# Order of the even mixer, low-rank gates in halves, and another bank for late sums in a tuned transformer kernel

## The reference, cut to what matters

```python
def first_block(...):
    layer 0: hn = rms_norm(h); proj = hn @ w_in_e
             a = gmlp_spatial_gate(gelu(a_uv), ...)        # u * (causal w_s @ layer_norm(v) + b_s)
             b = gated_deltanet(qkv, z, beta, a, ...)      # conv, silu, l2-norm of q and k,
                                                           # triangular solve, state over chunks,
                                                           # rms_norm per head, silu(z)
             h += concat([a, b]) @ w_out_e
    layer 1: h += diff_attention(hn @ w_qkv_o, ...) @ w_out_o   # 8 heads, two softmaxes each, norm per head
    each:    h += square(relu(rms_norm(h) @ w_mlp1)) @ w_mlp2
             h += (p @ w_ple_proj) * sigmoid(rms_norm(h) @ w_ple_gate)

def gla_mixer(h, w_in, w_gk_up, b_gk, head_norm, w_out):        # second block, layer 0
    q, k, v, glr, z = split(h @ w_in)                           # glr: 16 columns, the low rank
    gk = log_sigmoid(glr @ w_gk_up + b_gk) / 16                 # 16 x 512
    o = gla_chunked(q, k, v, gk)                                # 4 heads, 256 values each
    return (rms_norm(o, head_norm) * silu(z)) @ w_out
# second block, layer 1: nsa_mixer (untouched)
```

## Time and profile before

| | |
|---|---|
| median of 3 runs | 2063.66 us (2061.76 to 2064.04) |
| time of the profiled execution | 2062.59 us |
| its span | 2060.4 us |
| PE busy | 1980.1 us (96%) |
| DVE, ACT, POOL busy | 1069.3, 891.7, 221.5 us |
| chain that ended last | PE 78%, DVE 9%, ACT 7% |

### The profile page before, as it was taken

One profiled execution on the slowest core, in us unless ns is written; L12 is line 12 of the kernel. 1 busy time (PEld: TensorE's weight loads), 2 busy tenths in 40 slices (PEclk: granted clock), 3 DMA queues, 4 the chain that ended last, 5 costly groups with the idle time before them and its releaser, 6 DMA issues.

```text
span 2060.4 us, 27307 instructions
## 1 busy us (share of the span) xinstructions
PE 1980.1 (96%) x11161; PEld 1592.5 (77%) x11161; DVE 1069.3 (52%) x1706; ACT 891.7 (43%) x1659; POOL 221.5 (11%) x225
## 2 busy tenths in 40 slices
PE   7999989999999999999999999999999989999888
PEld 6778878888888788656888888887887778966567
DVE  5576555434434552566543434356535656555763
ACT  5562244323223563666442323256434442355562
POOL 1011000000000000342000000000000034233440
PEclk9999999999999999999999999999999999999999
DMA  4221013333232322111332333223221155611002
GB/s 146 81 76 48 22 62 99 96 102 101 84 102 82 102 77 97 62 41 42 93 103 85 99 102 102 82 83 97 82 92 62 62 149 147 177 42 42 1 1 72
DMA packets 122945, 169.94 MB, mean 82 GB/s; under 512 B 7562, under 2 KB 83862, under 8 KB 122822
## 3 DMA queue, kind: packets, MB, share of 16 engines
q1 hardware_dynamic: 114966, 151.00, 23.2%
q0 software_dynamic: 5504, 14.58, 2.6%
q10 hardware_dynamic: 2352, 2.62, 0.4%
HBM read 158.22 MB, written 2.10 MB: 78 GB/s over the span
## 4 chain that ended last, share of the span: by engine, by line
PE 78%; DVE 9%; ACT 7%; issue 2%; POOL 1%; DMA 1%; DVEq 0%; SPq 0%; ACTq 0%
PE PSUM L520 59%; PE PSUM L558 6%; PE PSUM L528 5%; DVE WL L413 2%; ACT XN L430 2%; PE PSUM L535 2%; ACT WH L486 1%; ACT TM L430 1%; DVE AR L413 1%; ACT AR L430 1%; PE PSUM L2557 1%; DVE AR L421 1%; PE PSUM L2606 1%; DVE XL L413 1%; PE PSUM L2578 1%
## 5 line engine op out<-in xcount | busy, mean ns | idle before, releaser
L413 DVE TENSOR_TENSOR WL<-RAW,WH 128x1024 fp32r<-128x1024 f32 (+2 forms) x284 | 348.9, 1230 | 383.7 <-ACT WH L486 383.2
L486 ACT CAST WH<-RAW 128x1024 fp32r<-128x1024 f32 (+2 forms) x284 | 293.2, 1035 | 372.2 <-PE PSUM L520 366.5
L520 PE MATMUL PSUM<-XH,WH 128*128 128x512 f32 (+3 forms) x1120 | 414.9, 370 | 10.5 <-DVE XL L413 6.7
L520 PE MATMUL PSUM<-XH,WL 128*128 128x512 f32 (+3 forms) x1120 | 407.3, 364 | 0.0
L520 PE MATMUL PSUM<-XL,WH 128*128 128x512 f32 (+3 forms) x1120 | 407.2, 364 | 0.0
L520 PE MATMUL PSUM<-WH,HP 128*128 128x512 f32 x1024 | 318.0, 390 | 1.9 <-DVE WL L413 1.9
L520 PE MATMUL PSUM<-WH,XH 128*128 128x512 f32 (+2 forms) x608 | 239.1, 393 | 11.7 <-DVE WL L413 5.5
L520 PEld LDWEIGHTS PSUM<-XH,WH 128*128 128x128 f32 (+2 forms) x1120 | 209.3, 187 | 50.7 <-DVE XL L413 8.4
L520 PEld LDWEIGHTS PSUM<-XL,WH 128*128 128x128 f32 (+2 forms) x1120 | 209.3, 187 | 35.8 <-issue 2.9
L520 PEld LDWEIGHTS PSUM<-XH,WL 128*128 128x128 f32 (+2 forms) x1120 | 209.0, 187 | 34.1
L520 PE MATMUL PSUM<-WH,XL 128*128 128x512 f32 (+2 forms) x608 | 232.0, 382 | 0.0
(11 more groups left out here) (236 smaller groups left out, 2480.4 us busy)
## 6 DMA issues: line engine op xcount, KB each, us to landing
RAW<-in_w_mlp_dram SPq DMA_DIRECT2D x64, 1024.0 KB, 5.2
RAW<-in_nsa_w_in_dram SPq DMA_DIRECT2D x13, 1024.0 KB, 5.5
RAW<-in_w_in_e_dram SPq DMA_DIRECT2D x12, 1024.0 KB, 5.2
RAW<-in_w_qkv_o_dram SPq DMA_DIRECT2D x12, 1024.0 KB, 5.2
RAW<-in_gla_w_in_dram SPq DMA_DIRECT2D x12, 1024.0 KB, 5.3
RAW<-in_w_ple_gate_dram SPq DMA_DIRECT2D x8, 1024.0 KB, 5.0
RAW<-in_w_out_e_dram SPq DMA_DIRECT2D x4, 1024.0 KB, 5.0
RAW<-in_w_out_o_dram SPq DMA_DIRECT2D x4, 1024.0 KB, 5.0
```

Source lines behind the costliest of these rows:

```text
L413: return x.do.tensor_tensor(o, a, b, op)
L486: a.do.copy(hi, r).then_inc(*up("w_hi", "w_hi", j))
L520: m = p.do.matmul(o, l, r, start=start and i == 0, stop=stop and i == len(pairs) - 1)
```

## The change

In the even mixer: `eu` 0 and 1 take the banks that `qkv(2, 3)` and `qkv(2, 2)` have left; gate 3 moves behind `eu` 0, and `vb` behind `eu` 1. The pieces between the levels are dealt 2, 2, 2, 1, 0 after each level and 2 more ahead of level 5, and DVE makes w27 (`first_part["ez", 3] + 3`) behind the low halves of the gate. In the head loop ACT makes w28 and w29 (`first_part["eg", 0] + 4`) ahead of `head_scale(0)`, DVE takes `head_gain` behind the next chunk's difference, and the last `gm_product` stands behind `head_norm(2)`. w32 is made within the loop of four half norms of `eo` 0, and no part more behind it. Two loads by POOL share a semaphore.

In the odd mixer `on` of the last key and `ovn` of heads 4 to 7 take bank 6.

In GLA the low rank's weights become unit "R": 80 columns, of which 0 to 15, 32 to 47 and 64 to 79 are loaded, each with the same 16 columns of the weight (the rest holds what the buffer held). The output rows are split so that one product of 80 rows in halves gives all three terms: `UPH` holds the upper weights' high half, high half and low half, `GLR` the gate's high half, low half and high half. The sum of both squares of a head is made by DVE (`sum_squares`), the matmul with ones is one per head, and `finish_head(h)` stands a head later, between the two projections `gz`.

```diff
@@ weight_plan
-    S(w, 2048, 2064)
+    plan.append(("R", rows(w)[:, :, 2048:2064]))
@@ sync_weights
+                if plan[u][0] == "R":
+                    for i in range(3):
+                        load(s, f"raw{u % NR}", ("raw", u) if i == 2 else (), raw_of(u)[:, :, 32 * i:32 * i + 16], plan[u][1])
+                    continue
@@ pe_even
-                if i in (8, 9):
-                    for g in (2 * i - 16, 2 * i - 15):
-                        pe_gate(p, g)
-            feat(p, ("eu", 0), EVEN)
+                if i == 8:
+                    pe_gate(p, 0)
+                    pe_gate(p, 1)
+                elif i == 9:
+                    pe_gate(p, 2)
+            feat(p, ("eu", 0), EVEN, bank=ps.where["qkv", 2, 3][0])
+            pe_gate(p, 3)
+            feat(p, ("eu", 1), EVEN, bank=ps.where["qkv", 2, 2][0])
             for n in range(4):
                 p.wait_ge(*at("qkv", 2, 3))
                 pe_token_form(p, "vb", n, VT)
-            feat(p, ("eu", 1), EVEN)
...
+                else:
+                    beside(2)
...
-                if lv <= 4:
-                    beside(3 if lv == 1 else 2)
+                beside((2, 2, 2, 1, 0)[lv - 1])
...
-                gm_product()
-                if n:
-                    head_norm(n - 1)
+                if n < 3:
+                    gm_product()
+                    if n:
+                        head_norm(n - 1)
                 within(n)
+            head_norm(2)
+            gm_product()
             head_norm(3)
@@ act_even
+                if n == 1:
+                    act_weights(a, first_part["eg", 0] + 4)
+                if n == 3:
+                    head_square(3)
                 if n:
                     head_scale(n - 1)
-                if n == 1:
-                    act_weights(a, first_part["eg", 0] + 4)
-            head_square(3)
...
                         act_half(a, MLP0, t)
+                        if t == 1:
+                            act_weights(a, j + 3)
@@ dve_even
             dve_gate(v, 2)
-            dve_gate(v, 3)
...
+            dve_gate(v, 3)
+            gate(0)
             for n in range(4):
                 dve_token_form(v, "vb", n, VB, beta)
-            gate(0)
...
-                if lv == 4:
-                    dve_weights(v, first_part["ez", 3] + 3)
...
+            dve_weights(v, first_part["ez", 3] + 3)
...
+                    if n > 1:
+                        head_gain(n - 2)
                     gm_add(*adds.pop(0))
...
                     for t in range(4):
                         add(t)
+                        if t == 2:
+                            dve_weights(v, j + 3)
                         dve_half(v, MLP0, t)
-                    dve_weights(v, j + 4)
@@ pe_odd
+        LATE = 4
-                several(p, ("ovn", h), lambda b: [(b[:, :], ONE, tm("ov", h))], bank=4)
+                several(p, ("ovn", h), lambda b: [(b[:, :], ONE, tm("ov", h))], bank=4 if h < LATE else 6)
-                    finish(*f, bank=4)
+                    finish(*f, bank=4 if f != o_feats[15] else 6)
@@ pe_gla
-                p.wait_ge(*at("gk_up"))
-                several(p, ("gup", h), lambda b: [(b[:, :], UP[:, 128 * h:128 * h + 128], GLR)])
+                p.wait_ge(*at("up_lo"))
+                several(p, ("gup", h), lambda b: [(b[:, :], UPH[:, 128 * h:128 * h + 128], GLR)])
...
-                p.do.matmul(PS[b][:, :], ONE, tm("gq", h, 0), start=True, stop=False)
-                p.do.matmul(PS[b][:, :], ONE, tm("gq", h, 1), start=False, stop=True).then_inc(*ps.filled("gn", h))
+                several(p, ("gn", h), lambda b: [(b[:, :], ONE, tm("gq", h, 0))])
...
                     feat(p, ("gz", 2 + 2 * h), GLA)
+                    if h:
+                        finish_head(h - 1)
                     feat(p, ("gz", 3 + 2 * h), GLA)
                     values(h + 1)
                 outputs(h)
-                if h < 3:
-                    finish_head(h)
+            finish_head(2)
@@ act_gla
+            a.wait_ge(*at("gk_up"))
+            a.do.copy(UPH, UP).then_inc(*up("gate_halves", "up_hi"))
+            a.wait_ge(*ps.full("gs"))
+            a.do.copy(GLR, bank("gs")[0:80, :]).then_inc(*up("gate_halves", "glr_hi"))
@@ dve_gla
-            v.do.tensor_copy(GLR, bank("gs")[0:16, :]).then_inc(*ps.read("gs"))
+            tt(v, UPH[THIRD, :], UP[THIRD, :], UPH[THIRD, :].bitcast(F32), ALU.subtract).then_inc(*up("up_lo", "up_lo"))
+            v.wait_ge(*at("glr_hi"))
+            tt(v, GLR[SECOND, :], bank("gs")[SECOND, :], GLR[SECOND, :].bitcast(F32), ALU.subtract).then_inc(*ps.read("gs"))
...
+            def sum_squares(h):
+                v.wait_ge(*at("gsq", h, 0))
+                v.wait_ge(*at("gsq", h, 1))
+                tt(v, tm("gq", h, 0), tm("gq", h, 0), tm("gq", h, 1), ALU.add).then_inc(*up("gsq_sum", "gsq_sum", h))
...
                     values(h + 1)
-                    finish_head(h)
+                sum_squares(h)
@@ pool_gla
+            g.wait_ge(*ps.full("pg", 1, 0, 0))
+            step(g, g.do.memset(UP, 0.0))
+            for i in range(3):
+                load(g, "gk_up", ("gk_up",) if i == 2 else (), UP[32 * i:32 * i + 16, :], I["gla_w_gk_up_2"][0])
```

More of the change, by code:

```diff
@@ L444, in bass_decoder_pair @@
         for u, (kind, *_) in enumerate(plan):
-            n = {"F": 2, "T": 2, "P": 2, "V": 2, "G": 2, "S": 1}[kind]
+            n = {"F": 2, "T": 2, "P": 2, "V": 2, "G": 2, "S": 1, "R": 1}[kind]
             parts += [(u, i, n) for i in range(n)]
@@ L1322, in z_gate @@
                 act(a, EZ[:, m, :], bank("ez", m)[:, :], ACT.Silu).then_inc(*ps.read("ez", m))
-                act_weights(a, first_part["ez", m] + 3)
+                if m < 3:
+                    act_weights(a, first_part["ez", m] + 3)
             def gate(m):
@@ L1340, in act_even @@
                     a.wait_ge(*at("centred"))
-                    act(a, sq, vg, ACT.Square).then_inc(*up("v_squared", "v_squared"))
+                    act(a, sq, vg, ACT.Square).then_inc(*up("v_spread", "v_squared"))
                 elif i == 4:
@@ L1347, in act_even @@
                     step(a, act(a, va, va, ACT.Ln, scale=1.0 / 128, bias=EPSC))
-                    act(a, va, va, ACT.Exp, scale=-0.5).then_inc(*up("v_scale", "v_scale"))
+                    act(a, va, va, ACT.Exp, scale=-0.5).then_inc(*up("v_spread", "v_scale"))
                     conv_silu(j, m)
@@ L1648, in dve_even @@
                     m.then_inc(*ps.read("sn", n))
-                gm_add(*adds.pop(0))
+                if n < 3:
+                    gm_add(*adds.pop(0))
                 if n > 1:
                     head_rest(n - 2)
-                if n:
-                    head_gain(n - 1)
+            head_gain(2)
             dve_weights(v, first_part["eg", 1] + 3)
+            gm_add(*adds.pop(0))
             head_rest(2)
@@ L1680, in pool_even @@
             load(g, "bs", ("bs",), BS, I["gmlp_bs"].rearrange("a g t -> a (g t)")[0].partition_broadcast(128))
-            load(g, "dt", ("dt",), ST[:, 8:12], I["gdn_dt_bias"][0].partition_broadcast(128))
-            load(g, "a_log", ("a_log",), ST[:, 12:16], I["gdn_a_log"][0].partition_broadcast(128))
+            load(g, "dt_a_log", (), ST[:, 8:12], I["gdn_dt_bias"][0].partition_broadcast(128))
+            load(g, "dt_a_log", ("dt_a_log",), ST[:, 12:16], I["gdn_a_log"][0].partition_broadcast(128))
             g.wait_ge(*at("c_more"))
@@ L2050, in bass_decoder_pair @@
         RS = CS[:, L_R:L_R + 512]
-        UP = slot(11)[0:16, 0:512]
-        GLR = slot(11)[0:16, 512:1024]
+        UP = slot(3)[0:80, 0:512]
+        UPH = PP[0:80, 0, 0, :]
+        GLR = PP[0:80, 0, 1, :]
+        SECOND, THIRD = slice(32, 48), slice(64, 80)
         PI = slot(11)[:, 1024:1536].bitcast(I32)
@@ L2118, in finish_head @@
             def finish_head(h):
-                p.wait_ge(*at("gsq", h, 1))
-                b = ps.take("gn", h)
-                p.wait_ge(*ps.empty("gn", h))
-                p.do.matmul(PS[b][:, :], ONE, tm("gq", h, 0), start=True, stop=False)
-                p.do.matmul(PS[b][:, :], ONE, tm("gq", h, 1), start=False, stop=True).then_inc(*ps.filled("gn", h))
+                p.wait_ge(*at("gsq_sum", h))
+                several(p, ("gn", h), lambda b: [(b[:, :], ONE, tm("gq", h, 0))])
             values(0)
@@ L2209, in act_gla @@
                     gz(2 + 2 * h)
+                    if h:
+                        finish_head(h - 1)
                     gz(3 + 2 * h)
                 outputs(h)
-                if h < 3:
-                    finish_head(h)
                 if h == 2:
-                    for m in range(6):
+                    for m in range(4):
                         place(m)
             j = first_part["yo", 0, 0]
+            finish_head(2)
+            place(4)
+            place(5)
             finish_head(3)
```

18 lines of the change are left out of this document (10 added, 8 removed).

## The result

The changed kernel takes 2037.36 us in the median (2037.13 to 2037.76), the kernel before in the same session 2062.71 (2060.13 to 2064.04). The ratio is 0.9879, with a 95% interval from 0.9862 to 0.9896: 25 us faster, where 24.3 were forecast.

A forecast was written before the change was run, and what follows sets the result against it. PE, busy 1980.1 of 2060.4 us, was taken as the bound. Savings of 13.0 (even mixer), 1.5 (odd mixer), 3.7 (low rank) and 6.1 (heads) sum to 24.3, so 2063.66 - 24.3 = 2039.4 us, range 2036.5 to 2043.

The forecast's parts named there:

- two prices: Used throughout: a low clock stretch costs 1.7 us; a removed wait is some 0.15 us more than its bracket shows.
- Gates: Even mixer: `eu` 0 ahead of gate 3 starts work 2.7 us earlier and removes the low stretch at 140.5; -4.1 us.
- Pieces and w27: Even mixer: PE's 1.20 us wait at 227.81, for DVE making w27 before the level's product, goes; -1.3 us.
- Head loop and tail: Even mixer: three head-loop waits go, -4.85 us; earlier w32 in the tail, with its low stretch, gives -2.75.
- The w32 term: Even mixer's tail: earlier w32 saves 2.5 us and 1.7 for the low stretch, less costs for w33 and w35; -2.75.
- The new wait for w33: First MLP's start: DVE now makes w33 between the norm's steps, where PE waits anyway; a cost of 1.1 us.
- Odd mixer: Last attention rounds: a second bank removes waits, but DVE and ACT are nearly full; -1.5 us, bounds 0 and -4.2.
- The sign given for it: Odd mixer's rounds: the changed kernel should show DVE behind PE's remaining waits; no size given.
- Low rank: GLA: four float32 products become cheaper, -2.6 us, and the low stretch at 1441 goes, -1.7; wider weights cost; sum -3.7.
- Heads: GLA: four float32 matmuls with ones go, 3.6 us, and stalls 3.4, less a new wait of 0.9; -6.1.
- The new wait for the last state: GLA: `outputs(3)` follows `values(3)` with only a projection less between and may wait; a cost of 0.9 us.
- The first rival: At 140, 301 and 1441 us the clock falls all the same, so 5.1 us comes back: 2044.5; chance 0.15.

The follow-up runs named there:

- w32_back: The changed kernel with w32 and w33 made behind the four half norms of `eo` 0 again; one execution, 2042.53 us.
- w28_back: The changed kernel with ACT's w28 and w29 behind `head_scale(0)` again, DVE's order as changed; one execution, 2040.75 us.
- odd_undone: The changed kernel with every late sum of the odd mixer in bank 4 again; 2039.83 us, 0.9884 of the kernel before.
- gate_back: The changed kernel with gate 3 ahead of `eu` 0 again, on PE and DVE; one execution, 2043.00 us.
- after_again: The changed kernel, unedited, profiled a second time; 2038.39 us, 0.9877 of the kernel before.
- gla_undone: The changed kernel with the GLA mixer as before the change; 2048.65 us, 0.9929 of the kernel before.
- even_undone: The changed kernel with the even mixer as before (order, banks, weights), except the shared POOL semaphore; 2050.74 us, 0.9936 of the kernel before.
- gup32: Two runs: the changed kernel with its low-rank products in float32, on 16 rows (2044.51 us) or all 80 (2041.95 us); one execution each.
- loads_sixteen: The changed kernel with sixteen loads of the low rank's weights in place of three, the others without bearing on the output; one execution, 2042.59 us.
- w33_early: The changed kernel with DVE making w33 directly behind the first sum of the second half of `eo`; 2036.91 us, 0.9871 of the kernel before.

## Why the prediction was right

**What bounds the kernel, and two prices.** A wait of PE was taken as its bracket and 0.15 us more, and that held where one alone was put back. Across the 2.37 of w32_back PE falls 2.48 us behind the changed kernel, and across the 1.76 of w28_back 1.90 behind odd_undone, which has the same code and clock there. A low stretch was taken as 1.7. While PE runs without waits it is that (`eu` 0 of gate_back loses 1.6), but 1.5 is left of the one at 231 at the first MLP, and nothing of the one at 1890: the matmul behind it, at 1894.54, waits for nothing, and in after_again, where the clock is 1.00, it has a wait for POOL that hides as much.

```profile
1896.02 1.09 PE L2625 MATMUL PSUM<-CB,AR 128*128 128x128 f32 x8 [1.50 <-POOL AR L413]
```

A float32 matmul with 512 columns was taken as 0.9 and measured 3.5 / 4 = 0.88.

**Gates.** 4.1 forecast; gate_back gives 3.7, the kernel before 4.0. By the parts, 3.45 less the 0.88 that PE now waits for the conv and 1.6 for the clock are 4.2. What is given back further on was sized at 0.2 and is 0.5 to 0.6.

**Pieces and w27.** 1.3 forecast and 5.0 - 4.0 = about 1.0 by the table; the wait itself is gone. That is by difference; no run puts w27 or the pieces back alone.

**Head loop and tail.** 7.6 forecast, 7.8 measured. The w32 term is shown (3.0 against 2.75). ACT's part of the head loop is shown with 2.4; that DVE's and PE's order give the rest is by difference only. The new wait for w33 was foreseen with 1.1 and is 2.08 - 0.79 = 1.3.

**Odd mixer.** 1.5 forecast between bounds of 0 and 4.2, 1.2 to 1.4 measured. That the bank is not all that bounds these rounds was read off the busy time of DVE and ACT, and held. The sign given for it held in part: DVE was to stand behind the waits that remain, and of the three it stands behind one and ACT behind two.

**Low rank.** 3.7 forecast. The products alone give 2.7 (3.63 to 0.93), the low stretch 1.6 (226.09 less the 224.52 of gla_undone), and the wider weights cost 0.4, by which the norm's turns come later (from 1407.08 to 1420.44 it was 13.36, from 1391.78 to 1405.57 it is 13.79). Together that is 3.9. The size was right; its reason only half: the forecast took the stretch as a part of these products, and gla_undone has them without it.

**Heads.** 6.1 forecast, 6.2 by gla_undone, and the matmuls' share was shown as 3.5. The new wait for the last state was counted with 0.9 and is 0.76. The share of each removed stall was not tested by itself.

**What was wrong.** The text said that the forecast would be wrong if low stretches were found at new places. They were, at 1890 and 1979, and the time still held. The sentence took for a sign of the edit what differs between executions.

The first rival, that the clock falls all the same, is half true. With gate 3 ahead of `eu` 0 three of three profiles have the stretch there (before, even_undone, gate_back), with gate 3 behind it none of eleven: this term is shown. The one behind the wait for w32 is there in three of three with the old place (before, even_undone, w32_back). But of the ten profiles with the new place and the wait of 2.1 at the MLP, five have one at 301 to 303 instead (gla_undone, odd_undone, both gup32, loads_sixteen). In four of these five the stretch at 231 is gone in exchange, so the total is firm where the place is not. From the first row to the one at 718.27 there are 600.9 to 601.1 us in seven of the eight profiles in which the even mixer is the changed kernel's, 602.6 in loads_sixteen, which has both stretches, and 613.9 in the kernel before. The third, behind the float32 products, came in two kernels with them of four.

That the whole came out so near is in part luck. Three stretches were booked as gone, 5 us; they went, and two new ones came, of which one costs 1.5 and the other nothing, while the start and the last mixer, which no edit touches, were 2.1 shorter by chance. Over the whole program the stretches did not become clearly fewer: four in the kernel before, two or three in the changed kernel, one to six in the other twelve (one of 6.8 us counted as two).

## What the runs showed of the hardware

The same wait, with the same length, is followed by the low clock in one execution and not in another. odd_undone has the changed kernel's even mixer unedited; it only began 1.5 us later:

```profile
231.97 0.50 PE L526 MATMUL PSUM<-WH,XH 128*128 128x512 f32 x1 [1.42 <-DVE XL L413]
...
232.00:235.50 3.50, 3.50 (x18) 2.96 (x19) 1.49 (x2) 1.25 (x4) 0.00 (x0) 1.00 0.00 0
...
302.00:305.00 3.00, 3.00 (x16) 3.00 (x16) 2.25 (x5) 2.90 (x7) 0.00 (x0) 0.50 0.43 106
```

The wait for the gate's low halves is 1.42 at 231.97, and the clock behind it is 1.00. In both profiles of the changed kernel the same wait, at 230.5 and 230.7, is followed by the low clock (0.56 from 231 to 234). In exchange odd_undone has 0.50 at 302, behind the wait of 2.09 at the MLP's start, where the changed kernel has 1.00. w28_back has neither, loads_sixteen both. Eleven profiles have the same order up to the wait of 1.42. The stretch is there in the six whose first row comes 117.09 to 117.79 us from the start, and not in the five where it comes at 117.91 to 118.73. The Trainium skill (TensorE: Matmul & The Clock Gate, Part 1: The HAM clock gate) says that throttled is the default and activity releases it; no run here contradicts that, and none tells which wait it will be. A stretch delays PE by 1.6 to 1.7 us at first, and between nothing and 1.5 is left at the end of the stage. Beside the program's start and end there were between one and six in a profile of these kernels. What decides the place was not settled; what could be seen is that it goes with a shift of the start by about a microsecond, which no edit here made. That the stretches are why runs of one kernel scatter by 1 to 3 us is not shown: two executions of the kernel before with the same mean clock, 0.996, took 2061.33 and 2065.98 us.

A load of 64 KB in 64-byte pieces lands 3.8 us behind its issue when it is alone, 3.9 in the median of three and 3.1 in the median of sixteen; sixteen in a row take some 12 us, 0.75 each.

## What to carry to other kernels

Cost an edit from the bracket of each wait that it removes, and look at what the engine behind it does next. Moving weight parts ahead of a table load or into a norm gave 2.4 and 3.0 us here, with no work removed, and the second left a wait for the next part, of which w33_early took 1.3 away. Where two other engines are nearly nine tenths busy, as in the attention rounds, do not book the waits' sum: here under a third of it came.

Price a low stretch of the clock as half its length at most, and book it to an edit only if several profiles have it at that place. Count how many such stretches a profile has, and compare stages between two rows of the same timeline, before reading a difference of 2 us between two executions as a gain.
